# Gate and up projections by Strassen's seven block products in a two-block transformer kernel

## The chip, the cores and the metric

The kernel runs on one core of a Trainium2 chip. The metric is the device time of one execution in microseconds (us), median over runs. All data are float32; the kernel reaches float32 accuracy by splitting each operand of a matmul into a high and a low part in the type fp32r and adding three products (high x high, high x low, low x high).

## The reference, cut to what matters

512 tokens of width 1024 pass through one hybrid block and then through two layers of a second kind. Each of these three ends in the same way, and only that end is touched by the change:

```python
x = x + merged @ w_out                 # 1024 x 1024
h2 = rmsnorm(x, norm2_g)
x = x + (silu(h2 @ w_gate) * (h2 @ w_up)) @ w_down     # w_gate, w_up 1024 x 2816, w_down 2816 x 1024
```

In the two later layers w_gate and w_up are the two halves of one matrix, w_ffn_in.

## The kernel before, in words

Activations are kept transposed: a tile of 128 features lies on 128 partitions, with the 512 tokens along a row. KT = 8 tiles make the width of 1024 and FT = 22 tiles the feed-forward width of 2816. A *chunk* is the weight block of one output tile: up to 8 blocks of 128x128. SyncE loads it (two DMAs) into one of four raw buffers `wraw`. It is then split into high and low in one of a few weight slots (`half(0)`, `half(1)`, `extra`), and TensorE multiplies it by 512-column moving operands in `chunk` (L1066): 3 matmuls for each of the 8 k tiles, so 24 of 512 columns each.

The *end stage* (`tail_pe`, `tail_dve`, `tail_act`, `down_splits`) runs three times, near 683 to 1086 us, 1434 to 1837 us and 2185 to 2587 us of the span. It has three parts:

1. The output projection, 8 chunks. VectorE adds each result to the residual `xT` (L1472), ScalarE makes the high part of the scaled `xT` and its square, VectorE makes the low part (L1474) and adds the square (L1479). The sum of squares gives the norm's scale `c_rs`.
2. Gate and up, 44 chunks, a gate chunk and an up chunk for each of the 22 tiles. VectorE drains each result with the scale (L1461), ScalarE applies silu, VectorE multiplies (L1966), and the product is split into `hid` by ScalarE (L2674) and VectorE (L1969) at once.
3. Down, 8 output tiles of three chunks (8, 8 and 6 k tiles).

In all three parts GpSimd splits the weights (`split`, named POOL in the profile): L743 writes the high part, L745 the low part. In the other stages of the two layers ScalarE (L2689) and VectorE (L2013) split them instead.

Every engine works its own queue in the order in which the program lists it; semaphores order the engines among each other. The counter `used` tells that TensorE has finished a chunk, `w_hi` and `w_lo` that a chunk's parts are written, `drained` that a PSUM tile is free. TensorE waits for `w_lo` of a chunk before it, and a slot is filled again only after `used` of the chunk that was in it.

Of the kernel before, what the change touches and what calls it, by code (L numbers as in the profile page):

```python
# [21 lines left out]
P = 128  # L22
# [18 lines left out]

C_KV, C_Q0, C_CK, C_Q1, C_CV, C_Q2, C_LRU, C_MIX, C_WO, C_GU, C_DN, C_B2 = np.cumsum(
    [0, 12, 1, 4, 1, 4, 6, 32, 16, 8, 44, 24]).tolist()
L_WO, L_GU, L_DN, C_LAYER = np.cumsum([52, 8, 44, 24]).tolist()
# [3 lines left out]
    [0, 8, 12, 2, 4, 6, 32, 16, 8, 44, 8]).tolist()  # L48
U_WO, U_GU, U_DN, T_LAYER = np.cumsum([56, 8, 44, 8]).tolist()
# [142 lines left out]
def build(nc, a, out):  # L192
    with ExitStack() as ctx:
# [163 lines left out]
        fg = pl(T)  # L357
        fu = pl(T)
        assert base + pl.at <= con2_at - 2 * KT * P * 4

# [9 lines left out]
        def half(h):  # L370
            return wsp[:, h].rearrange("p h k n -> p h (k n)")
# [5 lines left out]
        slots1 = [half(0), half(1), extra[:, :, :]]  # L377

# [94 lines left out]
        ff_act = steps("ffn_scalar", ["silu", "hi"])  # L473
        ff_dve = steps("ffn_vector", ["product", "lo"])
# [47 lines left out]
        def tail(stage, c0, wo, gate, up, down):  # L522

            stage(c0, 8, lambda i, s: wo(i * 4 * P + s * P))
            stage(c0 + 8, 2 * FT, lambda i, s: (up if s % 2 else gate)(i * 2 * P + (s // 2) * P))
            stage(c0 + 8 + 2 * FT, 24, lambda i, s: down(s % 3 * KT, i * 4 * P + (s // 3) * P), per=12)

        @block.sync
        def _(sp):
            def load(c, s, parts, dst=None, settle=False):  # L530

                if not isinstance(c, int) or c >= RAW:
                    sp.wait_ge(w_lo.sem, w_lo.at(c - RAW))
                    if settle:
                        settled(sp)
# [136 lines left out]
            def down(r, m):  # L672
# [3 lines left out]
            tail(stage, C_WO, lambda m: col_tile(a["w_out"][0], KT, m), lambda m: col_tile(a["w_gate"][0], KT, m),  # L676
                 lambda m: col_tile(a["w_up"][0], KT, m), down)
# [5 lines left out]
            wi2, wo2, wf2, wd2 = (stacked(x) for x in ("w_in_2", "w_out_2", "w_ffn_in_2", "w_ffn_out_2"))  # L683
            pw2 = a["pool_w_2"].rearrange("l g (k p) (m n) -> p (l g k) m n", p=P, n=P)
            with sp.Fori(0, LAYERS) as l:
# [43 lines left out]
                tail(stage, c0 + L_WO, lambda m: col2(wo2, m), lambda m: col2(wf2, m), lambda m: col2(wf2, m + DFF),  # L729
# [4 lines left out]
        def _(pool):  # L734
# [111 lines left out]
            for s in range(2, RAW):  # L846
                split(C_WO + s, C_WO // RAW, s)
            def down_splits(c, r):

                with pool.Fori(0, 2) as i:  # L850
# [3 lines left out]
            with pool.Fori(C_WO // RAW + 1, C_DN // RAW) as i:  # L854
                for s in range(RAW):
                    split(i * RAW + s, i, s)
            down_splits(C_DN, C_DN // RAW)
            with pool.Fori(0, LAYERS) as l:
                c0, r0 = l * C_LAYER + C_B2, l * (C_LAYER // RAW) + C_B2 // RAW
# [8 lines left out]
                for s in range(2, RAW):  # L868
                    split(c0 + (L_WO + s), r0 + L_WO // RAW, s)
                with pool.Fori(L_WO // RAW + 1, L_DN // RAW) as i:  # L870
                    for s in range(RAW):
                        split(c0 + i * RAW + s, i + r0, s)
                down_splits(c0 + L_DN, r0 + L_DN // RAW)

        def tail_pe(pe, chunk, free, proj, norm, split_by, c0, t0, src, ready, k, n, ff):


            with pe.Fori(0, 4) as i:
                for s in range(2):
                    proj(c0 + i * 2 + s, t0 + i * 2 + s, s, lambda h, kt: src[:, h, kt, :], None if s else ready)  # L880
            proj(c0 + 8, t0 + 8, 0, ready=split_by(res_dve, n))
            norm(k, n + 7)
            proj(c0 + 9, t0 + 9, 1)
            with pe.Fori(1, FT) as i:
# [1988 lines left out]
```

## Time and profile before

| what | value |
|---|---|
| median of three runs | 2599.03 us (2598.3 to 2599.88) |
| span of the profiled execution | 2597.4 us |
| busy, share of the span: TensorE | 98% |
| VectorE, ScalarE, GpSimd | 46%, 32%, 45% |
| mean granted TensorE clock | 0.986 |

The profiled execution is the hardware profiler's record of one run; its span is from its first instruction to its last, 1.6 us less than the median of the runs. A line such as L1066 is the line of the kernel before that issued the instruction. Busy time of TensorE (PE) counts overlapping matmuls once. GpSimd is POOL, VectorE is DVE, ScalarE is ACT.

### The profile page before, as it was taken

How to read it: one execution, taken by the hardware profiler on the slowest of the kernel's cores; microseconds unless marked ns; L12 is line 12 of the kernel's file. 1: busy time of each engine (PE TensorE's matmuls, PEld its weight loads, DVE VectorE, ACT ScalarE, POOL GpSimd, SP SyncE). 2: the span in 40 equal slices, each digit the busy share in tenths (PEclk: the TensorE clock that was granted, in tenths of full speed). 3: DMA queues.
4: the chain of work that ended last, by engine and by line, in shares of the span. 5: the costliest groups of instructions: out<-in, count | busy, mean ns of one | idle time of the engine just before them, and what ended most of it. 6: DMA issues, size and time to landing. Idle time of an engine off the chain costs nothing.

```text
span 2597.4 us, 37755 instructions
## 1 busy us (share of the span) xinstructions
PE 2538.9 (98%) x12947; PEld 2154.6 (83%) x12947; DVE 1200.3 (46%) x2275; ACT 834.5 (32%) x1473; POOL 1159.6 (45%) x586
## 2 busy tenths in 40 slices
PE   7999999999999999999999999999999999999998
PEld 6789988887888888899988888888899888888887
DVE  6567776664432221277775322211577765322211
ACT  4456655663211110144444211100244443211101
POOL 4335530000377788600000777788300002877885
PEclk8989989999999999999999999999999999999999
DMA  7321113332333333322232233333222222333332
GB/s 156 105 49 33 38 37 89 98 90 81 93 92 97 97 101 97 93 70 70 70 94 83 87 93 96 96 103 94 87 82 70 70 82 81 97 97 97 95 95 77
DMA packets 422189, 222.88 MB, mean 86 GB/s; under 512 B 59504, under 2 KB 420268, under 8 KB 422060
## 3 DMA queue, kind: packets, MB, share of 16 engines
q1 hardware_dynamic: 419100, 218.03, 29.6%
q10 hardware_dynamic: 2960, 3.22, 0.4%
q8 instruction: 71, 1.16, 0.2%
q14 instruction: 58, 0.48, 0.1%
HBM read 212.86 MB, written 2.10 MB: 83 GB/s over the span
## 4 chain that ended last, share of the span: by engine, by line
PE 88%; DVE 7%; ACT 3%; issue 2%; DMA 0%; DVEq 0%; ACTq 0%; POOL 0%
PE psA L1066 48%; PE psB L1089 13%; PE psA L1089 10%; PE psA L1322 5%; PE psB L1322 4%; PE psO L967 3%; PE psB L948 1%; PE psB L924 1%; DVE b L2013 1%; DVE b L2161 1%; DVE b L2053 0%; DVE b L1688 0%; DVE b L2034 0%; PE psO L1362 0%; DVE b L1672 0%
## 5 line engine op out<-in xcount | busy, mean ns | idle before, releaser
L1066 PE MATMUL psA<-b,b 128*128 128x512 f32 x5616 | 1288.0, 391 | 3.8 <-DVE b L1461 1.8
L1066 PEld LDWEIGHTS psA<-b,b 128*128 128x128 f32 x5616 | 1055.3, 188 | 234.5 <-issue 8.6
L743 POOL TENSOR_TENSOR b<-b,b 128x1024 fp32r<-128x1024 f32 x239 | 453.0, 1895 | 1202.5 <-PE psA L1066 1042.3
L745 POOL TENSOR_TENSOR b<-b,b 128x1024 fp32r<-128x1024 f32 x239 | 593.9, 2485 | 18.8
L1089 PE MATMUL psB<-b,b 128*128 128x512 f32 (+4 forms) x1626 | 367.3, 384 | 7.7 <-DVE b L1897 4.5
L1089 PEld LDWEIGHTS psB<-b,b 128*128 128x128 f32 (+2 forms) x1626 | 299.1, 195 | 68.1 <-DVE b L1897 4.9
L1089 PE MATMUL psA<-b,b 128*128 128x512 f32 x1356 | 324.4, 394 | 0.0
L1461 DVE SCALAR_TENSOR_TENSOR b<-psA,b 128x512 f32<-128x512 f32 x152 | 104.6, 690 | 461.6 <-PE psA L1066 457.7
L1089 PEld LDWEIGHTS psA<-b,b 128*128 128x128 f32 x1356 | 252.6, 188 | 54.4 <-issue 1.0
L1472 DVE TENSOR_TENSOR b<-b,psA 128x512 f32 x48 | 33.0, 688 | 337.9 <-PE psA L1066 337.9
L2347 ACT ACTIVATE b<-b,b (+1 forms) x56 | 40.6, 724 | 441.1 <-DVE b L1472 434.5
L2674 ACT ACTIVATE b<-psB 128x512 f32 x66 | 39.5, 598 | 370.3 <-DVE psB L1966 370.3
L1322 PE MATMUL psA<-b,b 128*128 128x256 f32 x1152 | 148.7, 288 | 2.2 <-DVE b L1472 2.2
L1322 PE MATMUL psB<-b,b 128*128 128x256 f32 x1152 | 147.8, 288 | 0.5 <-DVE b L2013 0.5
L1322 PEld LDWEIGHTS psA<-b,b 128*128 128x128 f32 x1152 | 143.7, 194 | 5.6 <-issue 4.9
L1322 PEld LDWEIGHTS psB<-b,b 128*128 128x128 f32 x1152 | 143.2, 194 | 2.7 <-issue 2.3
L2013 DVE TENSOR_TENSOR b<-b,b 128x1024 fp32r<-128x1024 f32 x102 | 124.4, 1220 | 13.7 <-ACT b L2689 13.7
L2689 ACT ACTIVATE b<-b 128x1024 fp32r<-128x1024 f32 x102 | 106.3, 1058 | 55.0 <-PE psA L1089 30.6
L2672 ACT ACTIVATE psB<-b 128x512 f32<-128x512 f32 x66 | 39.7, 602 | 251.9 <-DVE b L1461 251.9
L967 PE MATMUL psO<-b,b 128*128 128x128 f32 x640 | 83.3, 287 | 4.8 <-ACT b L2464 2.5
L967 PEld LDWEIGHTS psO<-b,b 128*128 128x128 f32 x640 | 79.5, 202 | 8.1 <-DVE b L1735 3.5
L2457 ACT ACTIVATE b<-b,b 128x512 f32<-128x512 f32 (+3 forms) x128 | 70.3, 551 | 45.1 <-DVE b L1681 45.1
(271 smaller groups left out, 2177.2 us busy)
## 6 DMA issues: line engine op xcount, KB each, us to landing
b<-in_w_in SPq DMA_DIRECT2D x296, 256.0 KB, 3.0
b<-in_w_ffn_in SPq DMA_DIRECT2D x176, 256.0 KB, 3.1
b<-in_w_ffn_out SPq DMA_DIRECT2D x64, 256.0 KB, 3.0
b<-in_w_out SPq DMA_DIRECT2D x48, 256.0 KB, 3.0
b<-in_w_gate SPq DMA_DIRECT2D x44, 256.0 KB, 3.1
b<-in_w_up SPq DMA_DIRECT2D x44, 256.0 KB, 3.2
b<-in_w_down SPq DMA_DIRECT2D x32, 256.0 KB, 3.0
b<-in_w_ffn_out SPq DMA_DIRECT2D x32, 192.0 KB, 2.6
```

The costliest lines, as they stand in the source:

```text
L743: nc.gpsimd.tensor_tensor(w[:, 0], wraw[:, s], ones[:, 0:1].broadcast_to([P, KT * P]), ALU.mult).then_inc(w_hi.sem, 1)
L745: nc.gpsimd.tensor_tensor(w[:, 1], wraw[:, s], hi_f(w[:, 0]), ALU.subtract).then_inc(w_lo.sem, 1)
L967: i = mm(psO[:, qt * P:(qt + 1) * P], PT[:, h, at:at + P], vtok[:, br, kt, n // 4, hd, :, :].rearrange("p h d -> p (h d)"), start=h == 0 a ...
L1066: i = mm(dst, w[:, wh, kt * P:(kt + 1) * P], rhs(xh, kt), start=first and kt == 0 and n == 0, stop=last and kt == kts - 1 and n == 2)
L1089: i = mm(dst, lh(x), rh(y), start=start and n == 0, stop=stop and n == 2, skip_group_check=skip)
L1322: i = mm(ring(t + q // 2)[:, q % 2 * V2:(q % 2 + 1) * V2], xg[:, xh, kt, q * P:(q + 1) * P], w[:, wh, k * V2:(k + 1) * V2], start=kt == 0 ...
L1461: v.scalar_tensor_tensor(dst, psA[:, s % 2, :], -0.5, c_rs[:, :], ALU.mult, ALU.mult).then_inc(drained.sem, 1)
L2013: v.tensor_tensor(w[:, 1], wraw[:, c % RAW], hi_f(w[:, 0]), ALU.subtract).then_inc(w_lo.sem, 1)
L2347: ac(flat(xg)[:, 0, bass.ds(m * T, T)], x, ACT.Copy, scale=gain).then_inc(res_act.sem, 1)
L2457: ac(pq, pq, ACT.Exp, bias=st[:, o + qt:o + 1 + qt], scale=-1.0, accum_out=st[:, o + 8 + qt:o + 9 + qt]).then_inc(ue_act.sem, 1)
L2672: ac(psS[:, 0, :], fg[:, :], ACT.Silu).then_inc(ff_act.sem, 1)
L2689: ac(w[:, 0], wraw[:, c % RAW], ACT.Copy).then_inc(w_hi.sem, 1)
```

## The change

Gate and up of two feed-forward tiles (a *quad*: 256 gate columns and 256 up columns) are computed together. The weights are taken as a 2x2 block matrix, gate and up as its two block columns and the even and odd k tiles as its two block rows. The activations are a 2x2 block matrix too, with tokens 0 to 255 and 256 to 511 in one direction. The product of the two is formed by Strassen's scheme (Winograd's variant) with seven block products in place of eight: A11, S1, A12, S4, S2, A22, S3. Each product is 24 matmuls of 256 columns. Eleven quads make the 22 tiles.

- Weights: SyncE loads a quad as four DMAs of 128x1024 into `wraw2` or `wraw`. GpSimd forms the four sums or differences of weights for S1 to S4 (`quad_sums`) and multiplies the up result by the scale (`quad_up`). ScalarE writes the high part of each of the seven operands (`hi`), VectorE the low part (`lo`).
- Activations: in the output projection ScalarE and VectorE build the seven right-hand operands, high and low (`even_operands`, `odd_operands`, `odd_lo`).
- Results: ScalarE copies two of the products, VectorE adds them up into gate and up (`gate_low`, `gate_high`, `up`), silu is over 1024 elements at once, and `product` writes the unsplit hidden pair `hid_raw`.
- Hidden split: `hid_raw` is split (`hidden_hi`, `hidden_lo`) at the end of gate and up, from the last quad on.
- GpSimd still splits six of the eight output chunks and all down chunks, now with three slots.

```diff
+            def quad_sums(c, g, q, loads):
+                raw = quad_raw(q)
+                pool.wait_ge(quad_in[q % 2], loads)
...
+                nc.gpsimd.tensor_tensor(sum1[:, :], raw[:, 2, :], raw[:, 3, :], ALU.add).then_inc(sa_pool.sem, 1)
...
+                nc.gpsimd.tensor_tensor(sum2[:, :], sum1[:, :], raw[:, 0, :], ALU.subtract).then_inc(sa_pool.sem, 1)
+                nc.gpsimd.tensor_tensor(raw[:, 2, :], raw[:, 0, :], raw[:, 2, :], ALU.subtract).then_inc(sa_pool.sem, 1)
...
+                pool.wait_ge(w_lo.sem, w_lo.at(c + SEVEN * q + S1))
+                settled(pool)
+                nc.gpsimd.tensor_tensor(sum1[:, :], raw[:, 1, :], sum2[:, :], ALU.subtract).then_inc(sa_pool.sem, 1)
+
+            def quad_up(g, q):
+                pool.wait_ge(fs_dve.sem, fs_dve.at(g + q, "c22"))
...
+            def quads(c, g, loads):
+                for q in range(QUADS):
+                    quad_sums(c, g, q, loads(q))
+                    if q:
+                        quad_up(g, q - 1)
...
+            def product(q, x):
+                pe.wait_ge(w_lo.sem, w_lo.at(c))
+                w = quad_slot(SEVEN * q + x)
+                for j in range(KT // 2):
+                    for p in range(2):
+                        at = (2 * j + p) * P
+                        for m, (wh, xh) in enumerate(((0, 0), (0, 1), (1, 0))):
+                            i = nc.tensor.matmul(banks[x][:, p * half_t:(p + 1) * half_t], w[:, wh, at:at + P], rhs[x][:, xh, j, :],
...
+                def odd_operands(j):
+                    v.tensor_tensor(odd_high[:, half_t:T], odd_high[:, 0:half_t], even2[:, half_t:T], ALU.subtract).then_inc(xo_dve.sem, 1)
...
+                    v.tensor_tensor(odd_high[:, T:T + half_t], odd_high[:, half_t:T], odd_low, ALU.subtract).then_inc(xo_dve.sem, 1)
...
+                def lo(c):
...
+                    v.tensor_tensor(w[:, 1], src[:, :], hi_f(w[:, 0]), ALU.subtract).then_inc(w_lo.sem, 1)
...
+                def gate_high(q):
+                    dve.wait_ge(used.sem, used.at(c1 + SEVEN * q + S2))
+                    step(v.tensor_tensor(u2, psA[:, 1, :], first_product, ALU.add))
+                    step(v.tensor_tensor(c12[:, :], psT[:, 1, :], u2, ALU.add))
...
+                def up(q):
+                    dve.wait_ge(used.sem, used.at(c1 + SEVEN * q + S3))
+                    step(v.tensor_tensor(u3[:, :], psA[:, 1, :], first_product, ALU.add))
...
+                    step(v.tensor_tensor(halves(up2, 1), pairs(fifth_product), pairs(u3[:, :]), ALU.add))
...
+                for q in range(QUADS):
+                    c = SEVEN * q
+                    if q:
+                        up(q - 1)
+                        lo(c + 2)
+                    lo(c + 3)
+                    if q:
+                        product(q - 1)
+                    lo(c + 4)
...
+                    gate_low(q)
+                    lo(c + 5)
...
+                    lo(c + 6)
...
+                    gate_high(q)
+                    lo(c + 7)
+                    lo(c + 8)
```

The order of GpSimd's queue, at the gate and up part of a layer. Before, it holds pairs of splits, here two of them (`b2_50` is the raw buffer, `b3_51` and `b71_119` the weight slots, `b5_53` a row of ones):

```order
L743 TENSOR_TENSOR b3_51<-b2_50,b5_53 128x1024
L744 REGISTER_ALU
L745 TENSOR_TENSOR b3_51<-b2_50,b3_51 128x1024
L743 TENSOR_TENSOR b71_119<-b2_50,b5_53 128x1024
L744 REGISTER_ALU
L745 TENSOR_TENSOR b71_119<-b2_50,b71_119 128x1024
```

Now, for each quad, it holds five additions or multiplications (`b97_145` raw, `b98_146` and `b95_143` the two sums, `b94_142` the up result, `b10_58` the scale):

```order
L917 TENSOR_TENSOR b98_146<-b97_145 128x1024
L918 ISA
L921 REGISTER_ALU
L923 TENSOR_TENSOR b95_143<-b98_146,b97_145 128x1024
L924 TENSOR_TENSOR b97_145<-b97_145 128x1024
L925 REGISTER_ALU
L927 REGISTER_ALU
L929 TENSOR_TENSOR b98_146<-b97_145,b95_143 128x1024
L933 ISA
L935 TENSOR_TENSOR b94_142<-b94_142,b10_58 128x1024
```

The splits have left GpSimd's queue for the length of this part, and two-input sums of the same size stand in their place.

VectorE's queue in the same part, before, for one feed-forward tile (`b93_141` and `b94_142` are the drained gate and up, `b92_140` is `hid`):

```order
L1461 SCALAR_TENSOR_TENSOR b93_141<-psA,b10_58 128x512
L1460 REGISTER_ALU
L1461 SCALAR_TENSOR_TENSOR b94_142<-psA,b10_58 128x512
L1964 ISA
L1965 ISA
L1966 TENSOR_TENSOR psB<-psB,b94_142 128x512
L1967 REGISTER_ALU
L1969 ISA
L1969 TENSOR_TENSOR b92_140<-psB,b92_140 128x512
```

Now, for one quad, from `up` of the quad before to `gate_high` (L2135 is `lo`, L2171 to L2174 `up`, L2184 `product`, L2158 `gate_low`, L2163 to L2167 `gate_high`; `b12_60` is the first product's copy, `b15_63` is u3):

```order
L2171 TENSOR_TENSOR b15_63<-psA,b12_60 128x512
L2173 SCALAR_TENSOR_TENSOR b94_142<-psB,b15_63 128x2x256
L2174 TENSOR_TENSOR b94_142<-b93_141,b15_63 128x2x256
L2135 TENSOR_TENSOR b3_51<-b97_145,b3_51 128x1024
L2135 TENSOR_TENSOR b71_119<-b98_146,b71_119 128x1024
L2184 SCALAR_TENSOR_TENSOR b93_141<-b94_142,psB 128x1024
L2135 TENSOR_TENSOR b3_51<-b95_143,b3_51 128x1024
L2158 SCALAR_TENSOR_TENSOR psB<-psA,b10_58 128x2x256
L2135 TENSOR_TENSOR b3_51<-b97_145,b3_51 128x1024
L2135 TENSOR_TENSOR b71_119<-b97_145,b71_119 128x1024
L2163 TENSOR_TENSOR b12_60<-psA,b12_60 128x512
L2165 TENSOR_TENSOR b13_61<-psB,b12_60 128x512
```

The weights' low parts have come onto VectorE. These seven (two more stand behind `gate_high`) and L2174 read two operands that both lie in SBUF; the others read one of theirs from PSUM (psA, psB).

VectorE's queue in the output projection, now, for a pair of chunks (`b1_49` is `xT`, `b96_144` and `b4_52` are the right-hand operands):

```order
L2098 TENSOR_TENSOR b1_49<-b1_49,psA 128x512
L2106 TENSOR_TENSOR b12_60<-b12_60 128x256
L2109 TENSOR_TENSOR b96_144<-b12_60,b96_144 128x2x256
L2102 TENSOR_TENSOR b11_59<-b11_59,psB 128x512
L2098 TENSOR_TENSOR b1_49<-b1_49,psA 128x512
L2113 TENSOR_TENSOR b94_142<-b94_142,b12_60 128x256
L2116 TENSOR_TENSOR b94_142<-b94_142,b12_60 128x256
L2117 TENSOR_TENSOR b94_142<-b94_142,b12_60 128x256
L2119 TENSOR_TENSOR b96_144<-b12_60,b96_144 128x256
L2102 TENSOR_TENSOR b11_59<-b11_59,psB 128x512
L2124 TENSOR_TENSOR b4_52<-b94_142,b4_52 128x4x256
```

Where two low-part operations (L1474) stood, seven operations with both inputs in SBUF stand now, and the next chunk's addition (L2098) is queued behind them.

## Rows read from the trace of the kernel before

**Rows 1.** The page: busy time, share of the span and instructions of each engine.
```profile
PE 2538.9 (98%) x12947; PEld 2154.6 (83%) x12947; DVE 1200.3 (46%) x2275; ACT 834.5 (32%) x1473; POOL 1159.6 (45%) x586
```
**Rows 2.** The chain, from 730 us to the first end stage's end: start, us, what.
```profile
735.18 350.08 PE psA L1066 x1536
```
**Rows 3.** Windows: the last two end stages, and an attention stage.
```profile
core 0: us, PE busy (x) PEld busy (x) DVE busy (x) ACT busy (x) POOL busy (x), PEclk, DMA share, GB/s
...
1434.00:1837.00 403.00, 401.38 (x1760) 329.56 (x1758) 94.99 (x137) 49.10 (x79) 332.78 (x153) 1.00 0.32 95
2185.00:2587.00 402.00, 401.20 (x1759) 329.48 (x1757) 94.36 (x137) 49.10 (x79) 323.65 (x148) 1.00 0.30 89
```
```profile
1849.00:1881.00 32.00, 31.73 (x216) 28.56 (x214) 24.37 (x69) 14.02 (x31) 0.00 (x0) 1.00 0.21 67
```
**Rows 4.** Timeline of gate and up: start, us, engine, line, what.
```profile
828.00 0.69 DVE L1461 SCALAR_TENSOR_TENSOR b<-psA,b 128x512 f32<-128x512 f32 x1 [2.34 <-PE psA L1066]
...
833.44 0.69 DVE L1461 SCALAR_TENSOR_TENSOR b<-psA,b 128x512 f32<-128x512 f32 x1 [4.75 <-PE psA L1066]
```
**Rows 5.** The chain in attention stages: 256-column and 128-column matmuls.
```profile
1888.93 2.87 PE psA L1322 x24
```
```profile
178.69 2.23 PE psO L967 x20
```
**Rows 6.** Lines: duration ns min/median/max, for single instructions.
```profile
L2013 DVE TENSOR_TENSOR b<-b,b x102: 1208/1218/1228, 1093.4 to 2176.1; 128x1024 fp32r<-128x1024 f32 x102
```
```profile
L2689 ACT ACTIVATE b<-b x102: 1041/1058/1087, 1092.3 to 2174.9; 128x1024 fp32r<-128x1024 f32 x102
```
```profile
L752 POOL TENSOR_TENSOR b<-b,b x8: 2372/2399/2417, 46.1 to 92.4; 128x1024 fp32r<-128x1024 f32 x8
```
```profile
L1474 DVE SCALAR_TENSOR_TENSOR b<-b,b,b x56: 736/756/1646, 9.8 to 2588.9; - x48, 128x512 fp32r<-128x512 f32 x8
```
```profile
L1966 DVE TENSOR_TENSOR psB<-psB,b x66: 698/700/700, 735.8 to 2466.5; 128x512 f32<-128x512 f32 x66
```
```profile
L2672 ACT ACTIVATE psB<-b x66: 602/602/603, 735.1 to 2460.8; 128x512 f32<-128x512 f32 x66
```
**Rows 7.** Timeline of the start, GpSimd and VectorE at once.
```profile
12.53 1.89 POOL L743 TENSOR_TENSOR b<-b,b 128x1024 fp32r<-128x1024 f32 x1 [12.09 <-DMA b<-in_w_in]
...
13.57 1.40 DVE L1474 SCALAR_TENSOR_TENSOR b<-b,b,b 128x512 fp32r<-128x512 f32 x1
...
14.50 2.68 POOL L745 TENSOR_TENSOR b<-b,b 128x1024 fp32r<-128x1024 f32 x1
14.89 0.67 DVE L1479 TENSOR_TENSOR b<-b,psB 128x512 f32<-128x512 f32 x1
...
16.09 1.64 DVE L1474 SCALAR_TENSOR_TENSOR b<-b,b,b 128x512 fp32r<-128x512 f32 x1
...
17.14 2.34 POOL L743 TENSOR_TENSOR b<-b,b 128x1024 fp32r<-128x1024 f32 x1
```
**Rows 8.** Timeline of the first output projection, the same two lines.
```profile
696.15 1.89 POOL L743 TENSOR_TENSOR b<-b,b 128x1024 fp32r<-128x1024 f32 x1 [0.92 <-PE psA L1066]
...
697.66 0.93 DVE L1474 SCALAR_TENSOR_TENSOR b<-b,b,b  x1 [1.14 <-ACT b L2347]
698.12 2.73 POOL L745 TENSOR_TENSOR b<-b,b 128x1024 fp32r<-128x1024 f32 x1
```
**Rows 9.** Timeline at 387 us, a 1024-element VectorE operation and a GpSimd one.
```profile
387.26 1.22 DVE L1818 TENSOR_TENSOR b<-b,b 128x1024 fp32r<-128x1024 f32 x1
387.42 1.53 POOL L807 TENSOR_TENSOR b<-b,b 128x256 f32<-128x256 f32 x1 [3.41 <-DVE b L1726]
```
**Rows 10.** GpSimd's groups by form: busy us, mean ns of one, idle before.
```profile
L807 POOL TENSOR_TENSOR b<-b,b 128x256 f32<-128x256 f32 x8 | 5.8, 730 | 11.6 <-DVE b L1726 11.6
L803 POOL TENSOR_TENSOR b<-b,b 128x256 f32<-128x256 f32 x8 | 4.9, 616 | 0.7
```

## What the change will do to the time, predicted

> **What bounds the kernel now.** I read the page first: TensorE is busy 98% of the span [rows 1]. The windows show the same for the end stages: 401.4 of 403 us and 401.2 of 402 us [rows 3]. The chain of waits has one piece of 350.08 us of matmuls in the first of them, 1,536 recorded [rows 2]. So a cut in TensorE's work there is worth its full length, if the other engines keep up. The timeline gives the pace: VectorE's drains, one a chunk, start at 828.00 and 833.44 us, so a chunk takes 5.44 us [rows 4], or 226.7 ns for each of its 24 matmuls. An end stage has 8 + 44 chunks and 8 x 22/8 = 22 more of down, 74 in all, 402.6 us. Gate and up are 44 x 5.44 = 239.4 us of them, 21.76 us for a quad.
>
> **TensorE's own part.** A quad becomes 7 x 24 = 168 matmuls of 256 columns in place of 96 of 512. Columns fall by an eighth, the number of matmuls rises by three quarters. The row for 24 matmuls of 256 columns in the attention stages is 2.87 us; I take 2.88 [rows 5]. A quad is then 7 x 2.88 = 20.16 us, 1.60 less than before, 17.6 us per stage and 53 us over three stages. As a bound on the fixed part of a matmul: 20 of 128 columns take 2.23 us, 111 ns each, so a shape that halves the columns again would gain nothing [rows 5].
>
> The Trainium skill, "TensorE: Matmul & The Clock Gate", section "Back-to-back issue gap", has N/2.4 + 2.5 ns for a lone matmul, 109 ns at 256 columns and 216 ns at 512. By it a stage would save 228 - 202 = 26 us, not 17.6. The rows are 11 ns above it in both shapes, so they decide.
>
> **The other engines, alone.** Per quad ScalarE has seven high parts of 1.06 us, silu over 1,024 elements at most as much, and two copies of 0.60 us: 9.7 us [rows 6]. GpSimd has five two-input operations over 1,024 elements, 2.40 us each by L752: 12.0 us [rows 6]. The trace has no plain sum of this size; the lower bound is L743, 1.89 us, whose second input is one repeated element [rows 7], but the sums read two full operands as L752 does, so I take 2.40. VectorE has seven low parts of 1.22 us (L2013), the 1,024-element product (1.22 by the same row), six operations of 0.69 to 0.70 that read PSUM, and L2174 (0.72, between L1966 and L1474): 14.7 us [rows 6]. All are below 20.16. DMA carries the same 2 MB a quad at 32% of its time [rows 3]. With nothing else, the queues laid out product by product leave TensorE unbroken: a slot is free 5.76 us before its next product is due, and the two parts take 2.3 us.
>
> **What they do to each other.** VectorE's operations with both inputs in SBUF and GpSimd's operations shut each other out. GpSimd's L743 runs from 12.53 to 14.42 us; VectorE's L1474, issued at 13.57, takes 1.40 us and ends at 14.97, which is 0.55 behind GpSimd's end. The next L745 is held in turn: 2.68 us, to 17.18. The L1474 issued at 16.09 ends at 17.73, again 0.55 behind, and L743 behind it takes 2.34 in place of 1.89 [rows 7]. At 697.66 us the same, 0.93 us with an end 0.55 behind GpSimd's 698.04 [rows 8]. At 387.42 a GpSimd operation takes 1.53 us, where L803 of the same form takes 0.62, behind a VectorE operation of 1.22 [rows 9, 10]. L1479, with one input in PSUM, takes its usual 0.67 in the middle of a GpSimd operation [rows 7]. The hold is nearly the whole instruction: a blocked GpSimd sum ends 2.2 us after the release, a blocked low part of 1,024 elements would end 1.09 after it (0.55 for 512, plus 512 elements at 1.22 - 0.69 = 0.54).
>
> Before, VectorE has one such operation (0.75 us) per output or down chunk and none in gate and up. In the layers, where VectorE does split weights, GpSimd runs nothing at all [rows 3]. The change puts both into one stretch. Per quad GpSimd holds 5 x 2.23 = 11.2 us and VectorE 7 x 1.09 + 0.55 = 8.2, together 19.3 of 20.16 us. That fits only if each starts as the other ends, and VectorE's other 5.4 us fall inside GpSimd's holds. Its queue is strictly in order, so they mostly don't.
>
> **One quad, laid out.** I go through the queues in the order shown, 0.03 to 0.05 us from engine to engine, and the one that has waited longer goes first. Time 0 is the start of A11. VectorE: `lo` of S1 to 1.9; u3 and c21 to 3.2; c22 waits 1.0 for GpSimd's fourth sum (1.9 to 4.35), ends 4.9; `lo` of A12 to 6.0; GpSimd's `quad_up`, waiting since 4.9, goes next, so `lo` of S4 waits 2.2, ends 9.35; product to 10.5; `lo` of S2 waits 1.2 for the first sum, ends 12.9; `gate_low` to 13.5; `lo` of A22 waits 1.8 for the second, ends 16.4; `lo` of S3 waits 2.2 for the third, ends 19.75; `gate_high` to 21.8; `lo` of the next A11 to 23.0, and the next S1's starts at 24.0. A quad is 23.3 us: 14.7 of work, 8.4 of waiting, little else. TensorE starts its products at 0, 2.9, 6.1, 9.4, 12.9, 16.5, 20.4 and 23.3. VectorE is now the bound. The first quad takes 1.3 more for the norm, the second 1.1 less, the last has no sums to wait for; gate and up come to 254.8 us (24.6 + 22.2 + 8 x 23.3, and 21.4 for the last), 15.4 more than before.
>
> **Output projection.** For an odd chunk VectorE now has four small operations (L2113 to L2119; 0.41 us, an estimate: 512 elements take 0.69 and 1,024 take 1.22, so 256 about 0.42) and a 1,024-element one. GpSimd, which has three slots and so runs without a break from chunk 3 on, stands before nearly each: four or five waits of 1.2 to 2.2 us. `added` of the next chunk is queued behind, and TensorE waits for it to free its PSUM half. In my layout chunk 4 starts 1.8 us late, chunk 6 another 6.7, and the first product waits 3.1 for the last even operands: +11.7 us.
>
> **Down.** From the last quad on, VectorE has eleven `hidden_lo` of 1.22 us, and GpSimd begins the down splits (L743 and L745) at once. Alone, VectorE stays ahead of TensorE, which takes 1.36 us for a pair of k tiles. With waits of 1.7 to 2.2 us in front of most, the first output tile takes 26.1 us in place of 14.96: +11.1.
>
> **Sum.** 11.7 + 15.4 + 11.1 = 38.2 us per stage, 115 over three. The profiled execution is 2597.4 us, the median 1.6 above; on the median this gives **2714 us**.
>
> **Rivals.**
>
> 1. *VectorE keeps the ports.* The rows never show two VectorE operations of this kind in direct succession while GpSimd waits. If VectorE's next one goes first, S4 and S3 don't wait 2.2 us each, a quad is 21.2 us (gate and up -3.2 us) and the edges are +7.8 and +9.2: 13.8 per stage, **2640 us**. For turns speaks the reverse case: GpSimd's next L743, issued at 17.14 while its L745 was still running, came after the L1474 that had waited since 16.09 [rows 7]. The point from which it decides for turns or not is this one rule. The Trainium skill, "SBUF — State Buffer", section "Who interferes with whom", says that whichever issues first gets the shared pair for the whole instruction; by that GpSimd, issued first, goes first, 2714. No run so far shows this side of it.
>
> 2. *Faster: the waits are hidden.* If VectorE and GpSimd overlap here, because the sums' holds are short or fall where VectorE is idle, TensorE alone counts. Then the layout gives 386.0 us a stage, 16.6 less (17.6 less the 1 us of the norm), **2549 us**. It decides from a quad below 21.76: the waits per quad would have to fall from 8.4 to under 6.9 us, and those at the edges too. Against it: every overlap in the rows shows the full wait.
>
> 3. *The clock falls.* TensorE is idle for 3 us of 23, in pieces under 1.1. If it were granted 1.2 GHz, 256 columns would take at least 213 ns, a product 5.1 us, a quad 36 us: over 3,000 us. In the attention stages, with gaps of their own, the granted clock is 1.00 [rows 3]. Small.
>
> The change does do what it says: 77 products stand for 88 in TensorE's queue.
>
> **How the numbers follow.** Turns: 0.62, with a range of its own of 2690 to 2738 (sums 0.05 us off the 2.40 move a quad by 0.25 and a stage by 2.7 us). At the lower bound for the sums, 1.89 us, the same layout gives 20.8 a quad and 413.3 a stage, 32 us over three stages, 2631; the range takes that in. VectorE first: 0.22, 2640 with 20 either way. Hidden: 0.12. Clock or a worse chain: 0.04. The range 2622 to 2738 leaves out the hidden case and the tails. A measurement tells 0.2%, 5 us, from no change. Faster 0.13, within it 0.02, slower 0.85.
>
> **What would show it.** Right: `lo` (L2135) at 2 to 3.4 us for most, beside 1.2 for a few; GpSimd's sums at up to 3.3; drains of a quad 23 us apart; TensorE waiting for L2135, L2163 and L2098. Wrong: `lo` at 1.22 throughout, or quads of 20.2. Rival 1: of two `lo` in succession the second never waits, and GpSimd's operations reach 4.5 us.

## The result, and the profile after

| | before | after |
|---|---|---|
| median | 2599.45 us (2598.3 to 2601.99, 4 runs) | 2720.97 us (2719.23 to 2722.76, 4 runs) |
| ratio | | 1.0466, 95% interval 1.0451 to 1.0481: slower |
| span of the profiled execution | 2597.4 us | 2720.3 us |
| mean granted TensorE clock | 0.986 | 0.978 |

The kernel became 121.5 us slower; 2714 was predicted. The page of the changed kernel first: busy time, share of the span and instructions of each engine, then the chain by engine, and the row of `lo`:

```profile
PE 2544.0 (94%) x15323; PEld 2244.4 (83%) x15323; DVE 1884.8 (69%) x2602; ACT 1119.4 (41%) x1752; POOL 1052.8 (39%) x484
...
PE 56%; DVE 28%; issue 10%; ACT 5%; DVEq 0%; DMA 0%; ACTq 0%; POOL 0%
...
L2135 DVE TENSOR_TENSOR b<-b,b 128x1024 fp32r<-128x1024 f32 x231 | 494.1, 2161 | 27.5 <-ACT b L2973 27.5
```

TensorE's share is down from 98% [rows 1], and the chain that ended last runs through VectorE for 28% of the span. "Issue" is time in which an engine waited for nothing that the profile shows; in gate and up most of it lies over a `lo` that GpSimd holds up (the chain has 2.41 us of it from 842.59 us; the timeline below has such a `lo` there). `lo` takes 2161 ns on average and 1218 was its price alone [rows 6]: 117 of the 231 take 1.2 us, nearly all others 2.6 to 3.4. GpSimd's five operations in gate and up of the first end stage show the same wait in their durations (count, busy us, mean ns, idle before):

```profile
L924 POOL TENSOR_TENSOR b<-b 128x1024 f32<-128x1024 f32 x10 | 33.3, 3326 | 0.0
L935 POOL TENSOR_TENSOR b<-b,b 128x1024 f32<-128x1024 f32 x10 | 32.1, 3213 | 7.3 <-DVE b L2174 5.1 <-DMA b<-in_w_up 2.2
L929 POOL TENSOR_TENSOR b<-b,b 128x1024 f32<-128x1024 f32 x10 | 24.1, 2408 | 67.0 <-DVE b L2135 67.0
L917 POOL TENSOR_TENSOR b<-b 128x1024 f32<-128x1024 f32 x9 | 21.7, 2410 | 11.6 <-DVE b L2135 11.6
```

A sum by itself takes 2.40 us, as L752 did [rows 6]; two of the five wait 0.8 to 0.9 more. The timeline of one quad, VectorE and GpSimd (start, us, engine, line, what):

```profile
828.38 0.68 DVE L2163 TENSOR_TENSOR b<-psA,b 128x512 f32<-128x512 f32 x1
...
836.85 4.55 DVE L2135 TENSOR_TENSOR b<-b,b 128x1024 fp32r<-128x1024 f32 x2
837.11 3.21 POOL L935 TENSOR_TENSOR b<-b,b 128x1024 f32<-128x1024 f32 x1 [0.73 <-DVE b L2174]
...
841.58 2.41 POOL L917 TENSOR_TENSOR b<-b 128x1024 f32<-128x1024 f32 x1 [1.26 <-DVE b L2135]
842.45 2.62 DVE L2135 TENSOR_TENSOR b<-b,b 128x1024 fp32r<-128x1024 f32 x1
845.00 0.69 DVE L2158 SCALAR_TENSOR_TENSOR psB<-psA,b 128x512 f32<-128x512 f32 x1
845.25 2.40 POOL L923 TENSOR_TENSOR b<-b,b 128x1024 f32<-128x1024 f32 x1 [1.26 <-DVE b L2135]
845.60 6.47 DVE L2135 TENSOR_TENSOR b<-b,b 128x1024 fp32r<-128x1024 f32 x2
847.61 3.38 POOL L924 TENSOR_TENSOR b<-b 128x1024 f32<-128x1024 f32 x1
852.00 0.68 DVE L2163 TENSOR_TENSOR b<-psA,b 128x512 f32<-128x512 f32 x1
```

From L2163 to L2163 a quad is 852.00 - 828.38 = 23.6 us; 21.76 was its time before and 23.3 the prediction. The two pairs of `lo` decide rival 1. The pair at 836.85 would take 2.35 us alone (two of 1.22 whose records overlap by 0.09). GpSimd's L935 comes at 837.11, during its first, ends at 840.32, and the second `lo` ends 1.08 us behind it, at 841.40: GpSimd went in between the two, for 2.2 us. At 847.61 it is the other way: GpSimd ends L923 at 847.65 and has L924 ready, but the `lo` that has waited since 845.60 goes first, and L924 takes 3.38.

The end stage by parts, us from the first matmul of the output projection to that of gate and up, from there to that of down, and from there to the last start, for the three stages (starts of matmuls in the timeline; my subtraction). Here are all runs, those of the next section too:

| kernel | output projection | gate and up | down |
|---|---|---|---|
| before | 43.6, 43.8, 43.8 | 241.0, 241.2, 241.2 | 121.1, 121.1, 121.1 |
| after | 56.0, 53.7, 56.5 | 259.0, 259.5, 259.0 | 132.3, 131.6, 131.5 |
| small sums | 49.5, 52.6, 50.3 | 222.7, 222.9, 222.8 | 131.8, 131.5, 131.3 |
| write only | 49.5, 52.5, 52.5 | 222.7, 222.9, 222.8 | 131.7, 131.5, 131.5 |
| low from PSUM | 53.0, 53.7, 56.4 | 224.6, 225.1, 225.2 | 132.4, 131.8, 131.7 |
| sums on VectorE | 52.9, 55.2, 53.6 | 225.6, 225.0, 225.3 | 131.5, 131.1, 131.8 |
| up on VectorE | 53.0, 53.7, 56.5 | 245.5, 245.7, 245.5 | 131.5, 131.8, 131.5 |
| down edge | 52.9, 53.6, 55.9 | 225.1, 224.8, 224.9 | 123.3, 123.3, 123.3 |
| both edges | 45.7, 46.0, 46.0 | 224.2, 224.4, 225.5 | 124.8, 123.3, 125.0 |

After is longer than before by 41.5, 38.8 and 40.9 us, together 121.2 of the 122.9 us between the two profiled spans: nearly the whole difference lies in the end stages. By part and on average these are 11.7, 18.0 and 10.8 us a stage, where 11.7, 15.4 and 11.1 were forecast. The longest waits of TensorE in the first stage (us in total, times, longest):

```profile
PE psA L1203 <- DVE b L2098: 8.6, 2, 6.6
PE psA L979 <- DVE b L2135: 7.6, 18, 0.8
PE psB L979 <- DVE b L2135: 7.2, 18, 0.6
PE psA L979 <- DVE b L2163: 7.0, 10, 0.8
PE psA L1203 <- DVE b L2189: 6.9, 3, 4.5
```

In gate and up these are waits of under a microsecond, about one at each product; in the output projection there are two, 2.06 and 6.57 us, before chunks 4 and 6, and in down the longest is 4.50 us, for `hidden_lo` (L2189). The small operations of an odd chunk in the output projection, by the timeline:

```profile
694.74 2.46 POOL L794 TENSOR_TENSOR b<-b,b 128x1024 fp32r<-128x1024 f32 x1
694.98 2.50 DVE L2116 TENSOR_TENSOR b<-b,b 128x256 f32<-128x256 f32 x1
697.15 2.08 POOL L792 TENSOR_TENSOR b<-b,b 128x1024 fp32r<-128x1024 f32 x1
697.40 2.11 DVE L2117 TENSOR_TENSOR b<-b,b 128x256 f32<-128x256 f32 x1
699.31 2.48 POOL L794 TENSOR_TENSOR b<-b,b 128x1024 fp32r<-128x1024 f32 x1
699.43 2.64 DVE L2119 TENSOR_TENSOR b<-b,b 128x256 fp32r<-128x256 f32 x1
```

L2113, of the same size, is issued at 694.50, just as GpSimd's L792 before these ends (694.67), and takes 0.43 us. With a whole GpSimd operation ahead of them the same 256 elements take 2.1 to 2.6 us.

### The profile page after: what moved, and what is told of

It is laid out like the page before. It is cut to its first block, busy times and chain, and to the rows that moved or that the text cites. A ratio compares the mean times of both kernels' runs of the same rounds, so it can differ in the third digit from the quotient of the medians.

```text
span 2720.3 us, 42121 instructions
## 1 busy us (share of the span) xinstructions
PE 2544.0 (94%) x15323; PEld 2244.4 (83%) x15323; DVE 1884.8 (69%) x2602; ACT 1119.4 (41%) x1752; POOL 1052.8 (39%) x484
## 4 chain that ended last, share of the span: by engine, by line
PE 56%; DVE 28%; issue 10%; ACT 5%; DVEq 0%; DMA 0%; ACTq 0%; POOL 0%
PE psA L1203 14%; PE psB L1226 12%; PE psA L1226 9%; DVE b L2135 9%; PE psA L1459 5%; PE psB L1459 4%; PE psA L979 3%; PE psO L1104 2%; DVE b L2174 2%; DVE b L2189 2%; PE psB L1085 1%; DVE b L2184 1%; PE psB L1061 1%; ACT b L2973 1%; DVE psB L2167 1%
## 5 line engine op out<-in xcount | busy, mean ns | idle before, releaser
L792 POOL TENSOR_TENSOR b<-b,b 128x1024 fp32r<-128x1024 f32 x107 | 214.4, 2004 | 1092.1 <-PE psA L1203 1011.8
L1203 PE MATMUL psA<-b,b 128*128 128x512 f32 x2448 | 586.1, 401 | 45.9 <-DVE b L2189 20.9
L1203 PEld LDWEIGHTS psA<-b,b 128*128 128x128 f32 x2448 | 468.6, 192 | 160.9 <-DVE b L2189 26.1
L2135 DVE TENSOR_TENSOR b<-b,b 128x1024 fp32r<-128x1024 f32 x231 | 494.1, 2161 | 27.5 <-ACT b L2973 27.5
L979 PE MATMUL psA<-b,b 128*128 128x256 f32 x3168 | 408.0, 287 | 48.9 <-DVE b L2163 24.0
L979 PEld LDWEIGHTS psA<-b,b 128*128 128x128 f32 x3168 | 388.2, 192 | 68.6 <-DVE b L2135 45.1
L2973 ACT ACTIVATE b<-b 128x1024 fp32r<-128x1024 f32 x231 | 240.8, 1056 | 208.7 <-PE psA L979 127.7
L979 PE MATMUL psB<-b,b 128*128 128x256 f32 x2376 | 304.1, 284 | 22.7 <-DVE b L2135 22.7
L1226 PE MATMUL psA<-b,b 128*128 128x512 f32 x1356 | 324.3, 394 | 0.0
L979 PEld LDWEIGHTS psB<-b,b 128*128 128x128 f32 x2376 | 289.4, 190 | 33.5 <-DVE b L2135 23.0
L1226 PEld LDWEIGHTS psA<-b,b 128*128 128x128 f32 x1356 | 252.5, 188 | 54.4 <-issue 1.0
L794 POOL TENSOR_TENSOR b<-b,b 128x1024 fp32r<-128x1024 f32 x107 | 280.3, 2620 | 8.4
L929 POOL TENSOR_TENSOR b<-b,b 128x1024 f32<-128x1024 f32 x33 | 79.4, 2406 | 239.3 <-DVE b L2135 239.3
L2613 ACT ACTIVATE b<-b,b (+1 forms) x32 | 23.1, 723 | 335.6 <-DVE b L1609 328.7
L1459 PE MATMUL psA<-b,b 128*128 128x256 f32 x1152 | 148.6, 288 | 2.0 <-DVE b L1609 2.0
L1459 PE MATMUL psB<-b,b 128*128 128x256 f32 x1152 | 147.8, 288 | 0.6 <-DVE b L2279 0.6
L1459 PEld LDWEIGHTS psA<-b,b 128*128 128x128 f32 x1152 | 143.5, 194 | 5.5 <-issue 4.8
L1459 PEld LDWEIGHTS psB<-b,b 128*128 128x128 f32 x1152 | 143.2, 194 | 2.7 <-issue 2.4
L2279 DVE TENSOR_TENSOR b<-b,b 128x1024 fp32r<-128x1024 f32 x102 | 124.5, 1220 | 14.8 <-ACT b L3043 12.4
```

Of the source, the lines that this page charges most:

```text
L792: nc.gpsimd.tensor_tensor(w[:, 0], wraw[:, s], ones[:, 0:1].broadcast_to([P, KT * P]), ALU.mult).then_inc(w_hi.sem, 1)
L794: nc.gpsimd.tensor_tensor(w[:, 1], wraw[:, s], hi_f(w[:, 0]), ALU.subtract).then_inc(w_lo.sem, 1)
L929: nc.gpsimd.tensor_tensor(sum1[:, :], raw[:, 1, :], sum2[:, :], ALU.subtract).then_inc(sa_pool.sem, 1)
L979: i = nc.tensor.matmul(banks[x][:, p * half_t:(p + 1) * half_t], w[:, wh, at:at + P], rhs[x][:, xh, j, :], start=first and j == 0 and p == ...
L1203: i = mm(dst, w[:, wh, kt * P:(kt + 1) * P], rhs(xh, kt), start=first and kt == 0 and n == 0, stop=last and kt == kts - 1 and n == 2)
L1226: i = mm(dst, lh(x), rh(y), start=start and n == 0, stop=stop and n == 2, skip_group_check=skip)
```

## The experiments

My theory: VectorE's operations with two inputs in SBUF and GpSimd's operations that read SBUF take turns, and this lengthens the quad and both edges. The rivals: VectorE simply has too many operations; the matmul of 256 columns saves less than it should; the wait is for writes as well as reads. The first three kernels below leave out or change part of the computation, as stated; the others compute all of it.

**Small sums.** GpSimd's five operations in gate and up shrink to 64 columns, and S1, S4 and S2 are read from the raw tiles (that part is not shown), so that the result lacks the sums. Their order and waits stay.

```diff
-                nc.gpsimd.tensor_tensor(sum1[:, :], raw[:, 2, :], raw[:, 3, :], ALU.add).then_inc(sa_pool.sem, 1)
+                nc.gpsimd.tensor_tensor(sum1[:, 0:64], raw[:, 2, 0:64], raw[:, 3, 0:64], ALU.add).then_inc(sa_pool.sem, 1)
```

> The changed kernel with GpSimd's four weight sums and the scaling of up cut to 64 columns (the products then use unsummed weights; the sums are left out of the computation). All waits and the work of the other engines stay. Turns at the SBUF ports (my theory): VectorE's low parts (L2135) fall back to 1.22 us in gate and up, a quad takes 20.2 us instead of 23.6, gate and up about 223 us a stage; output projection and down stay slow, since GpSimd still splits weights there; total about 2610 us. Rival, VectorE is simply loaded too full or the 256-column matmuls are too slow: a quad stays at 23 us or so, total 2700 us or more.

Measured: 2597.56 us, ratio to before 1.0002 (0.9991 to 1.0013). `lo` of the whole kernel (mean 1223 ns):

```profile
L2135 DVE TENSOR_TENSOR b<-b,b 128x1024 fp32r<-128x1024 f32 x231 | 282.0, 1223 | 137.5 <-ACT b L2973 137.5
```

VectorE now waits 137.5 us for ScalarE before `lo`: it has time to spare, with the same number of operations. Gate and up take 222.8 us a stage, 36.3 less than after. In all it is 123 us below after and lower than expected: the output projection is 4.6 us a stage shorter too, since the first quad's sums fall into it. Down is unchanged, as nothing in it was touched. The rival (a quad stays near 23 us, because VectorE is too full or matmuls of 256 columns are too slow) is out: from the third to the tenth, quads take 20.0 us.

**Write only.** The five become memsets over the full 1,024 elements, which write SBUF and read none of it; the sums and the scaling of up are left out.

```diff
-                nc.gpsimd.tensor_tensor(sum1[:, :], raw[:, 2, :], raw[:, 3, :], ALU.add).then_inc(sa_pool.sem, 1)
+                nc.gpsimd.memset(sum1[:, :], 0.01).then_inc(sa_pool.sem, 1)
```

> The changed kernel with each of GpSimd's four sums and the scaling replaced by a memset of the same 128x1024 tile: GpSimd writes SBUF and reads none (the sums are left out of the computation). If only GpSimd's reads collide with VectorE's second input, L2135 is 1.22 us even where it lies over a memset, a quad 20.2 us, total about 2610 us. Rival, any GpSimd access to SBUF shuts VectorE out: L2135 is longer wherever a memset (about 1 us, an estimate) lies over it, a quad 20.2 to 21.5 us.

Measured: 2598.03 us, ratio 1.0001 (0.9988 to 1.0013). GpSimd's memsets and `lo` in a stretch of gate and up:

```profile
L929 POOL MEMSET b<- 128x1024 f32 x9 | 8.6, 956 | 84.0 <-DVE b L2135 84.0
...
L917 POOL MEMSET b<- 128x1024 f32 x8 | 7.7, 957 | 21.8 <-DVE b L2135 21.8
```

```profile
L2135 DVE TENSOR_TENSOR b<-b,b 128x1024 fp32r<-128x1024 f32 x63 | 77.1, 1224 | 43.0 <-ACT b L2973 43.0
```

Both are at one constant duration: all 231 `lo` take 1215 to 1228 ns, although 60 of the 162 memsets run at the same time as one. (The total is again 12 us under the expected 2610, for the same reason as in small sums.) So writes of the full size don't hold up VectorE's operations here; what is left for the sums is that they read. The Trainium skill, "SBUF — State Buffer", section "Who interferes with whom", says just this: a VectorE instruction with two SBUF inputs contends with a GpSimd one that reads SBUF, not with one that only writes it. These runs agree.

**Low from PSUM.** The sums stay on GpSimd in full; `lo` takes one of its two inputs from PSUM (for all products but the first few), from data other than the high part.

```diff
+                    if c < 5:
+                        v.tensor_tensor(w[:, 1], src[:, :], hi_f(w[:, 0]), ALU.subtract).then_inc(w_lo.sem, 1)
+                    else:
+                        v.scalar_tensor_tensor(w[:, 1].rearrange("p (a t) -> p a t", a=2), src[:, :].rearrange("p (a t) -> p a t", a=2), 0.0,
+                                               psO[:, :].unsqueeze(1).broadcast_to([P, 2, T]), ALU.mult, ALU.mult).then_inc(w_lo.sem, 1)
```

> The changed kernel with GpSimd's sums at full size, and VectorE's low parts of all but the first five weight operands computed with one input in SBUF and one in PSUM (they come out zero, so the low part of the weights is left out of the computation). Same sizes, same waits, same number of instructions on both engines. Turns at the ports for two SBUF inputs: L2135 at 1.2 us, GpSimd's sums at 2.4, a quad 20.2 us, gate and up about 225 us a stage, total about 2630 us. Rival, the two engines slow each other whatever VectorE reads, or VectorE is too full: a quad stays above 22.5 us, total above 2690 us.

Measured: 2613.58 us, ratio 1.0062 (1.0039 to 1.0085). GpSimd's sums and VectorE's `lo` (here L2138), both with as much work as in after:

```profile
L917 POOL TENSOR_TENSOR b<-b 128x1024 f32<-128x1024 f32 x9 | 21.7, 2414 | 3.6 <-DVE b L2138 3.6
L924 POOL TENSOR_TENSOR b<-b 128x1024 f32<-128x1024 f32 x9 | 21.7, 2413 | 0.0
```

```profile
L2138 DVE SCALAR_TENSOR_TENSOR b<-b,psO 128x1024 fp32r<-128x1024 f32 x65 | 79.1, 1218 | 35.3 <-ACT b L2977 35.3
```

L924 falls from 3326 to 2413 ns and `lo` from a mean of 2161 to 1218; 147 of the 231 `lo` run beside a sum. So the count and size of the operations on both engines are not the cause, only where the inputs lie. The kind of VectorE's instruction has changed too, from TENSOR_TENSOR to SCALAR_TENSOR_TENSOR, but L1474 is of that kind as well and was held up when both of its inputs lay in SBUF [rows 7]. Gate and up are 225.0 us a stage, as expected. The total is 16 us under the expected 2630: 34 us less in three stages from 2721 is 2619 already.

**Sums on VectorE.** All four sums and the product with the scale go to VectorE, in the gaps between its `lo`; GpSimd does nothing in gate and up.

```diff
+                def s1(q):
+                    raw = quad_raw(q)
+                    dve.wait_ge(quad_in[q % 2], loads(q))
...
+                    v.tensor_tensor(sum1[:, :], raw[:, 2, :], raw[:, 3, :], ALU.add).then_inc(sa_pool.sem, 1)
```

> The changed kernel with the four sums and the scaling of up moved from GpSimd to VectorE, result unchanged. VectorE's work per quad grows from 14.7 to about 20.7 us, but nothing waits for ports any more. By the theory a quad is 20.2 to 21 us (an operation of 1.22 us on VectorE costs less than the 1.7 us of waiting that one on GpSimd brings on average), gate and up 225 to 232 us, total 2628 to 2650 us. Rival, VectorE's own load is what slowed the quad: it gets longer still, 23.6 + 6, and the total goes over 2850 us.

Measured: 2613.23 us, ratio 1.0059 (1.0036 to 1.0083), 108 us below after and 15 below the expected range, though gate and up, at 225.3 us, are inside theirs: the range of the total was added up too high, as in low from PSUM. VectorE has five operations more a quad than in after and gate and up take 34 us less. "VectorE has too many operations" is refuted: on average each of GpSimd's five operations cost more VectorE time (23.6 us a quad, less the 14.7 of VectorE's own work and the 0.9 that it waits for ScalarE, is 8.0, or 1.6 for each, a figure of my accounting) than the 1.22 us it costs VectorE to do it.

**Up on VectorE.** A dose of the same: only the product with the scale moves.

```diff
-                    if q:
-                        quad_up(g, q - 1)
...
                     if q < QUADS - 1:
+                        own(q, "c22")
+                        v.tensor_tensor(up2[:, :, :], up2[:, :, :], c_rs[:, :].unsqueeze(1).broadcast_to([P, 2, T]), ALU.mult).then_inc(fs_pool.sem, 1)
```

> The changed kernel with one thing moved: the product of the up pair with the reciprocal scale (128 x 512 pairs, read from two SBUF operands) goes from GpSimd to VectorE for quads 0 to 10, as it already is for quad 11; the four weight sums stay on GpSimd. The computation is whole. A dose of the same thing as the run with all sums on VectorE. The theory (GpSimd's operation holds SBUF for about 2.2 us of a quad in which VectorE is the bound; VectorE's own takes 1.2): 1.0 us less a quad, 23.6 to 22.6, times 33 quads is 33 us: 2688 (2680 to 2697). Rival A (VectorE is the bound by its count of operations, the turns are hidden): 1.2 us more a quad, +40: 2760. Rival B (the wait of the product for GpSimd was on the path, not the port): 2.2 us or more less a quad, under 2650.

There are eleven quads, so the expectation counts one too many: ten products move in each stage, 30 in all, and the theory's figure should read 2691. Measured: 2677.27 us, ratio 1.0303 (1.0286 to 1.0320), 44 us below after and 3 below the range given. Gate and up fall by 13.6 us a stage, 1.4 a quad, not 1.0. VectorE's rows in gate and up:

```profile
L2133 DVE TENSOR_TENSOR b<-b,b 128x1024 fp32r<-128x1024 f32 x72 | 132.8, 1865 | 9.1 <-ACT b L2973 9.1
...
L2177 DVE TENSOR_TENSOR b<-b,b 128x1024 f32<-128x1024 f32 x10 | 12.1, 1211 | 0.0
```

By the timeline of a quad its seven `lo` take 13.5 us in place of 16.1, and the product (L2177) adds 1.21. The pair that took 4.55 us takes 2.35, which is the 2.2 expected; the other 0.4 comes from the next `lo`, which takes 2.19 in place of 2.62, since GpSimd's sum of 2.41 us, which ends at 835.45, begins 1.3 us ahead of it (834.35) and not 0.87. So this one operation on GpSimd cost VectorE 2.6 us of a quad. The sign decides against rival A, the size, well under 2.2, against rival B.

**Down edge.** As "sums on VectorE", and ScalarE and VectorE split down chunks 0 to 3, GpSimd from chunk 4 on.

```diff
+                def lo_dn(s):
+                    dve.wait_ge(w_hi.sem, w_hi.at(c1 + SEVEN * QUADS + s))
+                    v.tensor_tensor(slots2[s % 3][:, 1], wraw[:, s % RAW], hi_f(slots2[s % 3][:, 0]), ALU.subtract).then_inc(w_lo.sem, 1)
...
-                pool.wait_ge(w_hi.sem, w_hi.at(c - 1))
+                pool.wait_ge(w_hi.sem, w_hi.at(c + 3))
```

> As the run with the sums on VectorE (2613 us), and also the first four down chunks (0 to 3) are split by ScalarE and VectorE, which have gate/up chunks to split no more by then; GpSimd splits from down chunk 4 on, and starts when all of chunk 3 is split. The computation is whole. In the run with the sums on VectorE the down projection's TensorE work takes 131.5 us to its last start where 119.5 to 120 would do with full matmuls throughout, so 11 to 12 us a stage are late there. The theory (GpSimd's splits of chunks 0 to 3 take turns at SBUF with VectorE's last gate/up work and with the drains): without them the wait is gone, down 120 to 123 us a stage, 9 to 11 us less a stage, together 2580 to 2586. Rival A (VectorE's own last work is what is late, whoever splits): VectorE has more to do, down stays at 131 or grows by 4 us a stage, together 2613 to 2625. Rival B (the fall of the clock at the edge is set by the change of matmul shape, not by idle time): the wait is gone but 3 to 4 us a stage stay, 2592.

Measured: 2584.93 us, ratio 0.9947 (0.9928 to 0.9966), 28 us below the run with the sums on VectorE. Down takes 123.3 us in each stage in place of 131.5, although VectorE has four operations more there. Rival A is out. Rival B is too: the matmuls change from 256 to 512 columns there as before, and the clock stays at 1.00:

```profile
core 0: us, PE busy (x) PEld busy (x) DVE busy (x) ACT busy (x) POOL busy (x), PEclk, DMA share, GB/s
...
966.00:1082.00 116.00, 114.15 (x497) 92.86 (x495) 25.40 (x29) 10.49 (x16) 96.02 (x44) 1.00 0.33 97
```

One thing the run does not separate: it also takes four chunks off an engine that splits them more slowly (4.3 us a chunk against 2.3). In "sums on VectorE" TensorE waited 0.4 and 0.3 us for a split of GpSimd (L794) there and 1.7, 4.5 and 0.4 for `hidden_lo`, so that part is small.

**Both edges.** The above, and output-projection chunks 2 to 7 are split by ScalarE and VectorE.

```diff
-            out_splits(C_WO, R_WO // RAW)
...
+                    w = m + 2
+                    if w < 8:
+                        dve.wait_ge(w_hi.sem, w_hi.at(c0 + w))
+                        v.tensor_tensor(slots_wo[w][:, 1], wraw[:, w % RAW], hi_f(slots_wo[w][:, 0]), ALU.subtract).then_inc(w_lo.sem, 1)
```

> As the run before it (down edge), and also output-projection chunks 2 to 7 are split by ScalarE and VectorE, so that GpSimd does nothing in the output projection. The computation is whole. The output projection's TensorE work is 52.9 us to gate/up's first matmul in the run with the sums on VectorE and 43.5 in the kernel before. The theory (turns at SBUF delay VectorE's chain of adds and squares there): 43.5 to 45 us, 8 to 9 us less a stage, so 25 to 28 us below the down-edge run; if both edges are as expected, 2553 to 2560, and the granted clock is 1.00 all through the stage. Rival A (VectorE is the bound there by its own work, since it takes two sums and two lo halves of the first quad in the same stretch): +3 to +6 us a stage, slower than the down-edge run by 9 to 18 us. Rival B (the splits are late, ScalarE's high halves of chunks 2 to 7 wait behind its squares): waits of TensorE for weights of 1 to 3 us a chunk, about as the down-edge run.

Measured: 2564.56 us (2562.95 to 2567.12), ratio 0.9863 (0.9846 to 0.9879): 156 us below after and 35 below before. The scheme gains, once GpSimd and VectorE don't read SBUF at once. The output projection is at 45.9 us, not at 43.5 to 45, and the total is 20 us below the down-edge run, not 25 to 28, and 5 us above the expected range. Rival A (slower than the down-edge run) is out, and so is rival B: TensorE waits for no split there, only for VectorE's `lo` and operands. The clock of 1.00 all through the stage did not come either: it falls for 3.4 us in down of the first and of the third stage (last section). Windows of the first stage, output projection, then gate and up without its first 17 us, then down:

```profile
core 0: us, PE busy (x) PEld busy (x) DVE busy (x) ACT busy (x) POOL busy (x), PEclk, DMA share, GB/s
682.00:727.80 45.80, 44.18 (x194) 35.97 (x193) 34.71 (x51) 24.58 (x37) 0.00 (x0) 1.00 0.40 125
...
745.00:950.00 205.00, 204.69 (x1720) 204.52 (x1719) 200.51 (x208) 98.72 (x106) 0.00 (x0) 1.00 0.33 103
950.00:1076.00 126.00, 124.15 (x543) 101.43 (x542) 34.18 (x38) 18.14 (x24) 94.81 (x44) 0.99 0.32 97
```

TensorE is again unbroken in gate and up, and VectorE is at 98%: another operation of 1.22 us a quad would make it the bound. What is left lies at the edges, and there VectorE's own load does count: TensorE waits 1.6 to 1.9 us for the first product, 1.2 to 2.6 at the norm, and 1.9 to 2.0 in down, where the `hidden_lo` stand behind `product` of the last quad; in two of three stages slower matmuls follow that last wait.

## Why the prediction was right

- **What bounds it.** TensorE before, VectorE after: right.
- **TensorE's part, 17.6 us a stage less.** Right: small sums shows gate and up at 222.8 against 241.1, 18.3 less; its undisturbed quads take 20.0 us (20.16 in the forecast), 119 ns for each matmul. The Trainium skill's figure for a lone matmul ("TensorE: Matmul & The Clock Gate", section "Back-to-back issue gap"), 109 ns at 256 columns, would have made 202 us; the traces disagree, and the lowest gate and up of any run is 222.7 us.
- **GpSimd's sum of two full operands, 2.40 us.** Right: 2.40 to 2.41.
- **The exclusion and its length.** Right: taken away by small sums, write only and low from PSUM, each in another way, with `lo` at 1.22 us. That only GpSimd's reads do it had not been claimed; write only shows it.
- **Turns.** Right: GpSimd goes between two `lo`, and `lo` between two sums, by the timeline above. Rival 1, VectorE first, is refuted: its quad of 21.2 us did not come and no GpSimd operation took 4.5 us.
- **One quad, 23.3 us.** 23.6: the mechanism was right, the sum 0.3 short. Pieces that show are L2174, 1.89 us where the layout has 1.72 (0.72 and a wait of 1.0), and the `lo` of S2 (2.62 against 2.4) and of A22 and S3 (6.47 against 6.25).
- **Gate and up, +15.4.** Measured 18.0, the term that was mis-sized. The first quad takes 25.2 us on average (24.6 in the layout), the second quad 22.6 (22.2), the next eight 23.6 each (23.3), the last 22.4 (21.4): 259.1 in place of 254.6 (to which the layout's own terms add up; it gives 254.8). Of these 4.5 us 1.7 don't count, since before has a norm of its own there and takes 241.1 us, not the 239.4 of 44 even chunks. The rest makes 8 us over three stages, all of the 7 between prediction and result.
- **Output projection, +11.7.** Measured 11.7 on average, but 12.4, 9.9 and 12.7, and that the average agrees to a tenth is luck. The waits before chunks 4 and 6 were forecast at 1.8 and 6.7 us and are 2.06 and 6.57 in the first stage, 2.16 and 6.58 in the third. The wait of 3.1 us for the first product is not there in the first stage and 0.58 in the third; instead TensorE ran slower ahead of it, at a lower clock (last section), and was as late for that. In the second stage chunk 4 waits 2.16 us, the clock is low behind it, chunk 6 does not wait at all, and the first product waits 5.67.
- **Down, +11.1.** Measured 10.8. The first output tile takes 26.4, 25.8 and 25.6 us in the three stages, forecast 26.1; all that follows takes 105.9 us, as before. Down edge shows that 8.2 of the excess go with GpSimd's splits; 2.2 stay, with a wait of 1.9 us for VectorE's own queue at the last quad.
- **Rival 2, hidden waits.** Refuted. **Rival 3, the clock.** It was put aside with "small", from windows in gate and up and attention. For gate and up that holds (1.00) from the second quad on. At the edges and in the first quad it doesn't: see the last section. Its cost is inside the terms above.

What stays open is how much of the edges' 22 us a stage is the clock and how much the waits alone. A bound, as an estimate from the clock records of after: in the two edges TensorE is busy for 11.9, 8.9 and 8.3 us of the three stages at the lower clock, and at the higher it would have needed half of that, so the clock is 4 to 6 us of the 22 at most.

## What to carry to other kernels

Look at where the inputs lie before giving GpSimd "free" elementwise work beside VectorE: a GpSimd operation that reads SBUF, next to a VectorE queue of operations with two SBUF inputs, cost VectorE 1.6 us on average here and 2.6 where it was moved alone, more than the 1.22 us of doing it there. A cut in TensorE's columns is worth its length only if the engines that feed it have that much room: here moving five operations a quad and the splits of ten chunks a stage turned +4.7% into -1.4%. Where two in-order queues contend, lay out one period by hand with the hold of each operation and the rule of turns; it came within 1.3% of the measured period, where the engines' own work (14.7 us of VectorE and 12.0 of GpSimd in a quad of 20.2) would not have shown it.

## What the hardware showed that I had not expected

TensorE's granted clock fell at the edges. Windows of the changed kernel around the wait of 6.57 us, before chunk 6, and around that of 1.93 us at the norm (us, TensorE busy, matmuls, granted clock, DMA):

```profile
core 0: us, PE busy (x), PEclk, DMA share, GB/s
...
717.00:721.00 4.00, 0.00 (x0) 0.75 0.79 241
721.00:724.00 3.00, 0.54 (x1) 0.50 1.10 349
724.00:728.00 4.00, 4.00 (x11) 0.50 0.07 22
728.00:732.00 4.00, 4.00 (x17) 0.84 0.00 0
732.00:736.00 4.00, 4.00 (x19) 1.00 0.00 2
746.00:748.00 2.00, 2.00 (x9) 0.58 0.00 0
748.00:750.00 2.00, 2.00 (x13) 0.57 0.00 0
```

TensorE does nothing from 716.9 to 723.5 us, and in that time the clock falls to its lower level of 1.2 GHz (0.50). Behind it 11 matmuls of 512 columns are recorded in 4 us, and 19 in the 4 us from 732 on, at 2.4 GHz (1.00). The product that starts at 746.02 takes 4.93 us, not 2.88. In down, after a wait of 4.50 us, the clock is 0.57 from 1012 to 1016 us and 0.58 from 1016 to 1020.

Behind waits of nearly the same length the clock fell once and once not. Both edges, first stage:

```profile
962.41 2.01 PE L1197 MATMUL psA<-b,b 128*128 128x512 f32 x5 [1.85 <-DVE b L2213]
```

Behind it the clock is 0.80 from 960 to 965 us and 0.86 from 965 to 970, and down takes 124.8 us. In the second stage of the same kernel, behind a wait of 1.97 us, it stays at 1.00 and down takes 123.3, as in all three stages of down edge. No run here tells what makes the difference.

A GpSimd memset of 1,024 elements beside `lo` takes 956 ns and leaves it at 1.22 us, where the sums cost it up to 2.2. In this run work on GpSimd that reads nothing from SBUF was free for VectorE; of other such work than memsets no run here tells.
